# Four column tiles of TensorE for the modulation products of a two-layer diffusion backbone

## What is computed

```
sh1, sc1, g1, sh2, sc2, g2 = split(silu(cond) @ w_mod + b_mod, 6)     # w_mod: 1024 x 6144
h  = rms_norm(x, norm1) * (1 + sc1) + sh1
x += g1 * (concat(neighbourhood attention, pooling, latent attention)(h @ w_in) @ w_out)
h2 = rms_norm(x, norm2) * (1 + sc2) + sh2
x += g2 * peer(h2)       # 8 heads x 16 experts a token, rows of peer_u and peer_v gathered
```

## Time and profile before

| | |
|---|---|
| time, median of 3 runs | 4233.54 us (4228.07 to 4234.6) |
| profiled execution, from first to last instruction | 4232.7 us |
| TensorE busy (matmul) | 3619.3 us, 86% |
| VectorE / ScalarE / GpSimd busy | 2552.9 / 959.9 / 2579.6 us |
| bytes moved | 1519.96 MB, mean 359 GB/s |
| mean granted TensorE clock | 0.971 of 2.4 GHz |

### The profile page before, as it was taken

How to read it: one execution, slowest core, us unless ns; L and a number is a source line. 1 busy time by engine, 2 the same in 40 slices (tenths; PEclk the granted TensorE clock), 3 DMA queues, 4 the chain that set the end, 5 groups by cost and what they waited for, 6 DMA issues and landing times.

```text
span 4232.7 us, 37599 instructions
## 1 busy us (share of the span) xinstructions
PE 3619.3 (86%) x10514; PEld 1683.3 (40%) x10514; DVE 2552.9 (60%) x6435; ACT 959.9 (23%) x2479; POOL 2579.6 (61%) x2833
## 2 busy tenths in 40 slices
PE   7899889989988888888887898999898887777777
PEld 3355444545434223444342355554443432222222
DVE  1275557767665446565656555677676666666664
ACT  1212222322211112222222222232231222221211
POOL 0057446666665556676667664566676677777776
PEclk9899999999999999999999999999999999999999
DMA  6477899999999999999999988999999999999999
GB/s 241 161 275 274 299 342 385 357 388 405 356 364 376 392 380 348 336 353 342 401 395 408 358 291 308 361 367 391 396 407 350 367 402 410 403 405 407 405 400 357
DMA packets 472276, 1519.96 MB, mean 359 GB/s; under 512 B 59996, under 2 KB 78720, under 8 KB 471560
## 3 DMA queue, kind: packets, MB, share of 16 engines
q0 software_dynamic: 368640, 1342.34, 82.2%
q1 hardware_dynamic: 103432, 175.21, 11.7%
HBM read 1511.71 MB, written 5.67 MB: 358 GB/s over the span
## 4 chain that ended last, share of the span: by engine, by line
PE 44%; DMA 26%; POOL 14%; issue 9%; DVE 4%; ACT 2%; SPq 1%; DVEq 0%; POOLq 0%; ACTq 0%
PE expert_sum L2125 23%; DMA expert_rows<-in_peer_v,experts 22%; POOL expert_rows L1042 13%; PE work L1884 4%; PE work L1858 3%; DMA expert_rows<-in_peer_u,experts 3%; PE work L2076 3%; PE work L2091 2%; PE work L2020 2%; PE work L2047 2%; PE work L1832 2%; DVE expert_rows L1792 2%; POOL stat_rstd L992 1%; PE work L2065 1%; PE work L1976 1%
## 5 line engine op out<-in xcount | busy, mean ns | idle before, releaser
L2125 PE MATMUL expert_sum<-expert_rows,weight_diagonals 128*128 128x512 f32 x5080 | 2475.9, 617 | 443.3 <-DMA expert_rows<-in_peer_v,experts 411.0
L1792 DVE CUSTOM_DVE_ANT_0 expert_rows<-expert_rows,tokens 128x1024 f32<-128x1024 f32 x1280 | 1556.2, 1216 | 844.0 <-DMA expert_rows<-in_peer_u,experts 838.2
L1042 POOL DMA_INDIRECT expert_rows<-in_peer_v,experts x1280 | 1231.1, 962 | 921.6 <-PE expert_sum L2125 713.7
L2125 PEld LDWEIGHTS expert_sum<-expert_rows,weight_diagonals 128*128 128x128 f32 x5080 | 906.2, 194 | 1671.6 <-issue 1359.3
L1042 POOL DMA_INDIRECT expert_rows<-in_peer_u,experts x1280 | 1214.1, 949 | 449.0 <-issue 353.7
L1326 ACT ACTIVATE weight_diagonals<-ident,expert_weights 128x128 f32<-128x128 f32 x1270 | 447.1, 392 | 579.1 <-PE expert_sum L2125 352.2
L1884 PE MATMUL work<-weight_ring,h_or_mixed 128*128 128x384 f32 (+3 forms) x800 | 250.6, 467 | 4.2 <-DMA weight_ring<-in_w_in 2.4
L1832 PE MATMUL work<-ident,scratch 128*128 128x128 f32 (+1 forms) x782 | 130.5, 290 | 96.1 <-DVE scratch L1422 37.0
L1884 PEld LDWEIGHTS work<-weight_ring,h_or_mixed 128*128 128x128 f32 x800 | 146.0, 193 | 109.5 <-issue 54.0
L1858 PE MATMUL work<-weight_ring,silu_cond 128*2 128x512 f32 x384 | 174.3, 608 | 11.6 <-DMA weight_ring<-in_w_mod 10.5
L1832 PEld LDWEIGHTS work<-ident,scratch 128*128 128x128 f32 (+1 forms) x782 | 99.3, 145 | 190.5 <-issue 73.4
(11 more groups left out here) (177 smaller groups left out, 2505.0 us busy)
## 6 DMA issues: line engine op xcount, KB each, us to landing
weight_ring<-in_w_mod SPq DMA_DIRECT2D x24, 2048.0 KB, 10.8
weight_ring<-in_w_out SPq DMA_DIRECT2D x16, 2048.0 KB, 18.0
weight_ring<-in_peer_wq SPq DMA_DIRECT2D x16, 2048.0 KB, 10.1
expert_rows<-in_peer_u,experts POOLq DMA_INDIRECT x1280, 7.3
expert_rows<-in_peer_v,experts POOLq DMA_INDIRECT x1280, 7.2
weight_ring<-in_w_in SPq DMA_DIRECT2D x12, 1536.0 KB, 10.9
weight_ring<-in_w_in SPq DMA_DIRECT2D x4, 2048.0 KB, 13.9
weight_ring<-in_t_pool SPq DMA_DIRECT2D x4, 2048.0 KB, 11.5
```

The source lines that it names most:

```text
L1042: g.indirect_dma_start(buffer, None, table, bass.IndirectOffsetOnAxis(ap=idx_st[:, col:col + 1], axis=0),).then_inc(row_in, 16)
L1792: v_.tensor_tensor_reduce(out=u_ring[r % U_RING], in0=u_ring[r % U_RING], in1=tokens[:, :], scale=1.0, scalar=0.0, op0=ALU.mult, op1=ALU.a ...
L2125: ins = t_.matmul(acc[:, hf * 512:(hf + 1) * 512], diags[:, at * P:(at + 1) * P], v_buffer(row)[:, hf * 512:(hf + 1) * 512], start=first = ...
```

## The change

The eight matmuls of a `mrow` go to four column tiles: matmul kk has tile kk mod 4 and writes rows 32q and 32q+1 of the bank, so each tile holds the sum of two of the eight, and the four partial sums lie in four places. They are joined later: `mcol` is now four ordinary float32 matmuls with a picker (`pick`, 128 x 2, ones in rows 0, 32, 64, 96 and in 1, 33, 65, 97) in place of the transposes, and `gate` uses a column of the picker in place of one of the identity. ScalarE copies all 128 rows to `mod_row`; VectorE adds all 128 rows to a quarter of the bias, which is therefore loaded into 128 partitions. VectorE clears the four banks of `work` at the start, and GpSimd makes the picker with three small additions. The `cost` of `mrow` in the weave goes from 7.0 to 3.0.

```diff
-    return {"mrow": 7.0, ...
+    return {"mrow": 3.0, ...
-        gate_rows = sb("gate_rows", 2 * D, parts=2)
+        gate_rows = sb("gate_rows", 2 * D)
+        pick = sb("quarter_picker", 2)
-        mod_row = SC[0:2, 2560:3072]
+        mod_row = SC[:, 2560:3072]
                 sp.dma_start(gate_rows[:, which * D:(which + 1) * D],
-                             b_mod[l, at:at + D].partition_broadcast(2)).then_inc(gate_bias_in[which], 16)
+                             b_mod[l, at:at + D].partition_broadcast(P)).then_inc(gate_bias_in[which], 16)
+            g.tensor_tensor(pick[:, :], ident[:, 0:2], ident[:, 32:34], ALU.add).then_inc(picker, 1)
+            for q in (2, 3):
+                pool.wait_ge(picker, q - 1)
+                g.tensor_tensor(pick[:, :], pick[:, :], ident[:, 32 * q:32 * q + 2], ALU.add).then_inc(picker, 1)
-                a_.activation(mod_row, bank(key)[0:2, :], ACT.Copy).then_inc(banks.frees(key), 1)
+                a_.activation(mod_row, bank(key), ACT.Copy).then_inc(banks.frees(key), 1)
+                    for i in range(4):
+                        v_.memset(work[:, i, :], 0.0).then_inc(work_cleared, 1)
+                quarter = 1.0 / MOD_TILES
-                v_.tensor_tensor(row, bank(key)[0:2, :], row, ALU.add).then_inc(banks.frees(key), 1)
+                v_.scalar_tensor_tensor(out=row, in0=row, scalar=quarter, in1=bank(key), op0=ALU.mult,
+                                        op1=ALU.add).then_inc(banks.frees(key), 1)
+                    pe.wait_ge(work_cleared, 4)
+                cond = sct[:, :].rearrange("p (c k) -> p k c", c=2)
                 for kk in range(KC):
-                    ins = t_.matmul(dst[0:2, :], sct[:, :].rearrange("p (c k) -> p k c", c=2)[:, kk, :], wt[:, kk, :],
-                                    start=kk == 0, stop=kk == KC - 1)
+                    q = kk % MOD_TILES
+                    ins = t_.matmul(dst[32 * q:32 * q + 2, :], cond[:, kk, :], wt[:, kk, :], start=kk < MOD_TILES,
+                                    stop=kk >= KC - MOD_TILES, tile_position=(0, 32 * q))
+                pe.wait_ge(picker, 3)
-                    ins = t_.transpose(dst[:, col:col + 2], mod_row[:, g * P:(g + 1) * P], ident[0:2, 0:2])
+                    ins = t_.matmul(dst[:, col:col + 2], mod_row[:, g * P:(g + 1) * P], pick[:, :], start=True,
+                                    stop=True)
-                t_.matmul(dst, ident[0:2, cnd:cnd + 1].broadcast_to([2, P]), gate_rows[:, at:at + 512],
+                t_.matmul(dst, pick[:, cnd:cnd + 1].broadcast_to([P, P]), gate_rows[:, at:at + 512],
                           start=True, stop=True).then_inc(banks.fills(key), 1)
```

More of the change, by code:

```diff
@@ L43 @@
 SLOTS = 2
+MOD_TILES = 4
 GROUP = ((0,), (1, 2, 3, 4))
@@ L210, in cost @@
         return 7.0 if step[2] else 0.5
-    return {"mrow": 7.0, "nT": 1.8, "tu": 0.7, "ct": 0.7, "cq": 0.4, "up": 2.0, "uT": 1.3, "ck": 0.3, "kp": 1.3,
+    return {"mrow": 3.0, "nT": 1.8, "tu": 0.7, "ct": 0.7, "cq": 0.4, "up": 2.0, "uT": 1.3, "ck": 0.3, "kp": 1.3,
             "kT": 1.3, "py": 0.4, "pp": 3.5, "s": 1.0, "pt": 1.0, "pv": 0.6, "ot": 1.8, "o": 8.8}.get(kind, 0.2)
@@ L721, in build @@
         ROWS_CLEARED, IDENT_CLEARED, IDENTITY, SKT_CLEARED, IOTA_I, SET_UP = 2, 3, 5, 7, 8, 9
+        work_cleared, picker = sem("work_cleared"), sem("picker_step")
         silu_done, vec_cols = sem("silu_done"), sem("vec_cols")
```

## The result

| | median us | lowest to highest | runs |
|---|---|---|---|
| before | 4234.6 | 4228.07 to 4251.34 | 5 |
| after | 4170.77 | 4168.96 to 4173.63 | 5 |

The ratio is 0.984, 95% interval 0.982 to 0.986: 64 us less, where 28 were forecast.

What follows compares the result with a forecast made beforehand. Transfers bound stretches of expert rows alone; TensorE nearly fills the weaves with attention and projections. Terms -3.1 - 15.1 - 2 - 7 + 2.6 - 3 = -27.6 from 4232.7 gave 4205.1, predicted as 4206 us, range 4190 to 4230.

Steps and rivals of the forecast that it cites:

- the products in the weaves: Shorter products in both weaves: -2 for layer 0's m10 and m11, -7 for layer 1's ten, -3 for its m10, m11.
- The additions: Bias load 2.0 and turning 1.0 in m0 to m3, turning of m9 0.5, layer 1's bias loads 2.6 us.
- The opening: Layer 0's m0 to m9, before any expert rows: -3.1 us for m0 to m3 and -15.1 for m4 to m9.
- The product's length: Within each product: tiles overlap partly, starts staying in program order, so 4.03 us instead of 7.03, 3.0 less.
- side by side: Rival: all four tiles run fully beside each other, 1.88 us a product, -36.5, 4197 us; chance 0.17.
- the first part: m0 to m3 of layer 0: m2 starts at 38.4, first projection wants its chunk at 53.5, -3.1 us.
- m4 to m9: Later opening of layer 0: loads become the bound, m9 ends at 139.6 instead of 155.2, -15.1 us after its turning.
- The new weights only move steps by a few rows; nothing: Weaves: the lower cost of a product shifts steps by a few rows only, gain 0.
- Layer 1's ten: Ten products in layer 1's weave, transfer share 0.98 against 1.03: -7 of at most 12.3 us.
- cover given back: Rival: bias load costs its full 2.7, waits drop the clock before m6 to m9; 4221 us, chance 0.15.
- no overlap: Rival: a product stays at 7.03 us, leaving only what the change adds, +8.6; 4242 us, chance 0.10.
- exposed switches: Rival: inside products, no overlap and every tile switch paid, 11.7 us a product; 4288 us, chance 0.08.

Runs made afterwards that it cites:

- pairs: Kernel after with the two matmuls of each tile behind one another in the program (tile kk // 2 instead of kk mod 4): 4174.7 us, ratio 0.9859.
- Cost7: Kernel after with the weave's cost of a product put back from 3.0 to 7.0: 4190.43 us, ratio to before 0.9893.
- tiles_opening: Kernel after with four tiles only for m0 to m9 of layer 0, the other 14 products in one tile: 4192.59 us, ratio 0.9903.
- split_halves: Kernel before with each of layer 1's twelve products cut into two steps of four matmuls, no tiles: 4225.08 us, ratio 0.9982.
- bias_two_rows: Kernel after with the gate's bias loaded into rows 0 and 1 only, other rows cleared, whole bias added: 4167.59 us, ratio 0.9843.
- one_tile: Kernel after with all eight matmuls of a product in one column tile, additions and order kept: 4225.14 us, ratio 0.997.
- before_cost3: Kernel before with the weave's cost of a product at 3.0 and nothing else: 4222.34 us, ratio 0.9965.
- late_x: bias_two_rows with gains and constants loaded behind m3's chunk, gate bias, cached keys and x behind the heads' chunks: 4342.92 us on a slower chip, ratio 0.984.

## Why the prediction was wrong

Three steps failed, all towards too small a gain. The order's term was put at nothing and measured 15 to 20 us; the products in the weaves were priced at 12 us and measured 27; the product itself was taken at 4.03 us and measured 1.90, which is worth some 8 us (two tiles against four). The additions cost 2 to 3 us where the sum held 6.1 for them (2.0 + 1.0 + 0.5 + 2.6). The opening came out as forecast: 18.5 us at the first expert row, against 3.1 + 15.1.

**The product's length: wrong.** The step was that matmuls start in the order of the program also across tiles, as all untiled ones of the trace do, so that a second half holds up the next tile: 4.03 us. Measured: 1.90, against the lower bound of 1.88, and 1.92 with a tile's instructions one behind the other in the program. The rival "side by side" had the right mechanism. The Trainium skill ("TensorE: Matmul & The Clock Gate", Part 3, What overlaps and what doesn't) holds that matmuls never start out of order; `pairs` contradicts it for different tiles: by the rule its product would take 12 x 0.43 + 0.59 = 5.75 us. The speed-up is 7.03 / 1.90 = 3.7. The Trainium skill ("TensorEngine Tiling (Array Packing)", Key Properties) speaks of a drain at each change of tiling mode. The traces show no time for it beyond what untiled products pay: where an expert row's matmul comes right ahead of a product, its start lies 0.52 us before the product's at the full clock, in the kernel before and in the kernel after alike.

**The opening: right in place and sum, with errors that cancel.** In the profile after, m2 starts at 39.00 (38.4 forecast) and the first projection at 54.96 (53.5): the first part gives 1.7 instead of 3.1. This is that one execution's clock, which was at the lower level through m3 and its turning. Cost7, pairs and tiles_opening have the same program here (pairs but for the tiles' order); in them m3 runs in 1.90 to 1.92 us and the first projection starts at 53.4 to 53.5, as forecast; in pairs and cost7 it then waits 4.6 us for its chunk, which was forecast to land at 53.3. m9 ends at 136.67 (139.6 less the 3.1 of m0 to m3, 136.5, was forecast), and at 135.3 to 137.3 in these three. m4 to m9 thus give 16.8 instead of 15.1, bound by their loads as said: m6 waits 5.05 us for its chunk. The product is shorter than forecast at the full clock, but of the ten only m5 and m9 ran wholly at it, and m6 to m8 took 3.2 to 3.6 us. The side-by-side rival, with nearly the right length (1.88), had 21.5 here.

**"The new weights only move steps by a few rows; nothing": wrong.** This term of the sum measured -15 us without the tiles and -20 with them, the largest miss of mechanism. In a weave the place of every step follows from sums of costs, so a changed cost shifts what stands behind it up to the end of that weave; and in the old order at least one meeting of steps left TensorE idle and the gathers behind. Which meetings the rest of it comes from, above all in layer 1, stays open; single profiled executions differ too much to tell.

**Layer 1's ten: right mechanism, term too small.** Forecast 7 of a ceiling of 12.3 (share 0.98 against 1.03), measured some 12: about the whole ceiling, with the share at 1.02 after. That holds of 7 us are what starves the gathers is shown by split_halves and by the share behind each product. Together with m10 and m11 of both layers, the products in the weaves bring 27 us, where 12 were forecast (2 + 7 + 3); how the other 15 divide between m10 and m11 of the two layers no run tells.

**What the change adds: over-priced.** 8.6 forecast for bias, turnings and copies together; measured 2 to 3 over the whole kernel, unclear from none. The 2.4 us of m2's delay is real. The +2.6 in layer 1 is not seen, but it is smaller than the 6 us by which profiles differ in that stage (bias_two_rows gains 16.9 there and the kernel after 16.0). In the opening one_tile is 6.6 us behind before_cost3 at row 0 (-8.9 against -2.3, 5 forecast), of which 1.2 are the clock, lower for longer in m2 (9.79 us instead of 8.55); and split_halves, with the opening of before, is 5.5 behind there, so that this difference is not told from none either.

By ratios, the 68 us (0.016 x 4236) divide into 28 for the tiles in the opening, 27 for the tiles in the weaves and 15 for the order, less 2 for the additions. The first two were measured with the new order; with the old one the change as a whole gains 45 (cost7), so the parts need not add up alike in another order.

The rivals: "cover given back" had the lower clock in m6 to m8 right, but m4 to m9 gained 16.8 us and not its 9; "no overlap" and "exposed switches" are refuted by the product's length.

## What to carry to other kernels

The float32 matmuls of this case (128 x 2 stationary, 128 x 512 moving) in four column tiles took a quarter of the instructions' time, 1.90 of 7.03 us, in both orders that were tried, and in two tiles half of it, 3.60; for such shapes the lower bound is the price to start from. What they bring is then read from what else is late, and a short list of loads may cap it. In a pipeline fed by gathers, price a long block of TensorE by how long it holds the queue, not by its share of the total: here, cutting it in two gained 8 to 11 us. A planner's cost is an edit of its own, to be timed alone before a gain is put down to the operation beside it.

## What the hardware showed that was not expected

In the profile after, TensorE's clock is at the lower level for longer in the opening. Stretches of 10 us of the kernel after and then of before; the number before the share is the granted clock (1.00 is 2.4 GHz, 0.50 is 1.2 GHz):

```profile
30.00:40.00 10.00, 1.00 (x8) 0.29 (x12) 0.00 (x0) 0.00 (x0) 0.00 (x0) 0.51 1.06 377
40.00:50.00 10.00, 8.39 (x43) 2.81 (x31) 0.00 (x0) 1.19 (x2) 0.00 (x0) 0.50 1.04 395
50.00:60.00 10.00, 8.25 (x23) 5.66 (x24) 1.80 (x7) 1.51 (x4) 0.00 (x0) 0.50 0.60 210
```

```profile
30.00:40.00 10.00, 4.91 (x13) 0.99 (x11) 0.00 (x0) 0.59 (x1) 0.00 (x0) 0.83 1.05 388
40.00:50.00 10.00, 9.32 (x26) 1.94 (x24) 0.00 (x0) 0.59 (x1) 0.00 (x0) 1.00 0.94 348
```

Before, the clock rose within m2; after, it is at the lower level from the wait ahead of m2 into the first projection, and m2, m3 and their turnings run at half speed (3.60 and 1.84 us instead of 1.90 and 1.02). They lie on the path to the first projection, so this takes back part of what the tiles give there. But it is no rule that short products keep the clock low: in pairs, cost7 and tiles_opening, whose products here are as short, m2 takes 3.5 to 3.6 us too, but m3 1.90 to 1.92, and the first projection starts 1.5 us earlier. With long products too the moment differs: m2 takes 8.31 us in before, 9.1 in split_halves, which has the same program there, and 9.79 in one_tile. One profile does not tell how soon the clock rises.

Chips differ: on the one of late_x the kernel before takes 4.3% longer, and where expert rows run alone the transfers reach 372 GB/s, against 404 for the kernel after over the same stretch on another chip:

```profile
3500.00:3600.00 100.00, 73.62 (x155) 26.75 (x153) 60.79 (x156) 18.82 (x44) 67.64 (x72) 0.97 0.98 372
```
